# A blocked triangular inverse in which the matrix engine's level loop starts half a level later

## The chip, the cores and the metric

The kernel runs on one core of one Trainium2 chip. The metric is the device time of one execution in microseconds. Before the change it is 2102.54 us, the median of 3 runs (2102.18 to 2102.79).

## The reference

A decoder trunk of two layers over 512 positions of width 1024: in each layer a half-weighted SwiGLU feed-forward, a mixer, and a second feed-forward. The even layer's mixer joins a gated linear recurrence with RWKV-7 time mixing. The latter keeps a matrix state for each of 8 heads of width 64:

```
def step(state, inp):
    r_t, w_t, k_t, v_t, kk_t, a_t = inp
    sa = einsum('bhvk,bhk->bhv', state, kk_t)
    state = (state * w_t[:, :, None, :] - sa[..., None] * (kk_t * a_t)[:, :, None, :]
             + v_t[..., None] * k_t[:, :, None, :])
    return state, einsum('bhvk,bhk->bhv', state, r_t)
```

The odd layer's mixer is a gated delta rule, which the change doesn't touch.

## The kernel before

The RWKV recurrence is computed in 8 chunks of 64 tokens. In a chunk it needs the inverse of a unit lower triangular 64x64 matrix, for 8 heads and 8 chunks. Heads go in two **rounds** (`q` = 0, 1) of two **streams** (`z` = 0, 1); a stream is one 128x512 tile, that is 16 blocks of 64x64 with two heads across the partitions. The inverse is built by doubling: **levels** of block size 2, 4, ... 64. A level of a stream is this chain:

- TensorE, `pe_level_u` (products at L725): 32 products 64x64 of the running inverse `XX` with the triangle `TM`, into the lower half of two PSUM banks;
- VectorE, `level_masked` (L2065): the result times a mask, into `IU`; ahead of it on VectorE stands `turned_across` (L2055 and L2057), three transposes of `XX` into `XT`;
- TensorE, `pe_level_xx` (L735): 32 products of `XT` and `IU`, into the upper half of the banks;
- ScalarE, `level_copied` (L1396): the copy of these into `XX`. The next level's products and transposes wait for it.

The last level has `pe_last_xx` (L744) in place of the second product. In the text u(z,l) and x(z,l) are the two products of stream z at level l.

Beside this chain TensorE does other products of the same round: `back_product` (L882), the **inner products** `inside_inner` (L891) and the **outer products** `inside_outer` (L902; these use banks 2 and 3 for stream 0, 6 and 7 for stream 1). ScalarE copies the outer results away in two copies for each stream (`inside_copied`, L1403), and signals `token_read`. In the loop TensorE also turns a staged tile of keys (`tokens_turned`, L692, called T(l) here) into the lower half of banks 2 and 3, so it first waits for `token_read[0]`; ScalarE copies that (`tokens_copied`, L1391), and GpSimd stages the next tile (`stage`, L1915). In round 0 ScalarE has two more copies in each of levels 1 and 2 (`branch_hi`, L1386).

The order on every engine is written out by hand, once for both rounds. TensorE's, from the middle of a round: back product 0, u(0,1), first x of stream 1, back product 1, inner 0, inner 1, outer 0, outer 1, wait for `token_read[0]`; then a hardware loop over l = 1 to 3 (`pe.Fori`) of u(1,l), x(0,l), T(l), u(0,l+1), x(1,l). ScalarE copies the results of the first x products, then inside 0 and inside 1, and then goes through the levels. VectorE's order isn't changed. After the rounds comes a scan over the chunks, whose first products wait for the last copies of both streams. Each 64x64 product is two instructions, a weight load and a matmul. TensorE's code outside `Fori` loops is straight-line.

Of the kernel before, what the change touches and what calls it, by code (L numbers as in the profile page):

```python
# [147 lines left out]
def hybrid_trunk_kernel(nc, x, params, const, w_gate, w_up, w_down, ab_in, ab_out, lru_a, lru_x,  # L148
# [28 lines left out]
    with ExitStack() as ctx:  # L177
# [423 lines left out]
        def _(pe):  # L601
# [87 lines left out]
            def tokens_turned(first, src, b, upper, across):  # L689

                for r, a, c in four_ways:
                    tr = pe.matmul(head_block(first, a if across else r, c, upper), src[r, b, c * CHUNK:(c + 1) * CHUNK],  # L692
                                   con("ident")[r, r], start=True, stop=True)
                tr.then_inc(tr_mm, 1)
# [24 lines left out]
            def pe_level_u(q, z, l):  # L719

                w = INV[z]
                pe.wait_ge(xx_read[z], 5 * q + l)
                pe.sem_inc(level_begun, 1)
                for a, f, c in four_ways:
                    mm = pe.matmul(head_block(4 * z, f, c), w["TM"][a, c, :], w["XX"][a, c, :], start=True, stop=True)  # L725
                mm.then_inc(u_mm[z], 1)

            def pe_level_xx(q, z, l):

                w = INV[z]  # L730
                pe.wait_ge(iu_ready[z], 5 * q + l + 1)
                pe.wait_ge(xt_turned[z], 4 * q + l)
                pe.sem_inc(level_begun, 1)
                for a, f, c in four_ways:
                    mm = pe.matmul(head_block(4 * z, a, c, upper=True), w["XT"][f, c, :], w["IU"][f, c, :], start=True, stop=True)  # L735
                mm.then_inc(xx_mm[z], 1)

            def pe_last_xx(q, z):
# [5 lines left out]
                    mm = pe.matmul(head_block(4 * z, crossed(r) if z else r, c, upper=True), w["IU"][r, c, :], w["XT"][r, c, :], start=True, stop=True)  # L744
                mm.then_inc(xx_mm[z], 1)

            def mix_out(phase, ready):

                n, c = norm_of[phase], base[phase] + AB_BLOCKS

                def rows_of(m, rows, wait):

                    more = (MORE_HI[:, m - 2], MORE_LO[:, m - 2]) if m in (2, 3) else None
                    unit(BANK[4 + m] if m < 4 else DOWN[m % 2], c + m, 0, (MIX_HI, MIX_LO), rows, rows[0] == 0, rows[-1] == KB - 1,
                         ready=ready if wait else None, at_col=rows[0], done=rows[-1] == KB - 1, weights=more)

                pe.wait_ge(logs_ready, 4)
                for m in range(4):
                    rows_of(m, range(4), m == 0)
                for m in range(2):  # L760
                    rows_of(m, (4, 5, 6), m == 0)
                for m in range(2):
                    rows_of(m, (7,), m == 0)
                for m in range(2, 4):
                    rows_of(m, range(4, KB), False)
                for m in range(4, KB):
                    pe.wait_ge(x_ready[m % 2], KB // 2 * (n + 1) + (m // 2 if m >= 6 else 1))
                    rows_of(m, range(KB), False)

            for phase in plan:  # L770
                if phase.startswith("ffn"):
                    q = ffn_index[phase] * (FB // 2)
# [17 lines left out]
                if phase == "ab":  # L790
# [94 lines left out]
                    def inside_inner(q, z):  # L885

                        b = 2 * q + z
                        pe.wait_ge(mat_ready[z], 4 * q + 4)
                        for r, a, c in four_ways:
                            cc = slice(c * CHUNK, (c + 1) * CHUNK)  # L890
                            mm = pe.matmul(head_block(4 * z + 2, crossed(r) if z else r, c), TKM[z][a, c, :], VT[a, b, cc], start=True, stop=True)  # L891
                        if z:
                            mm.then_inc(inner_mm, 1)
# [11 lines left out]
                    for q in range(2):  # L905
                        if q == 0:
                            triangle_product(0, 0)
                            triangle_product(0, 1)
                        if q == 0:
                            key_products(q, 0)  # L910
                            key_products(q, 1)
                            pe.wait_ge(bv_ready, 2)
                            tokens_turned(4, KF, 0, upper=False, across=True)
                            pe_first_u(q, 0)
                        else:
                            pe_first_u(q, 0)
                            key_products(q, 0)
                            key_products(q, 1)
                            pe.wait_ge(xx_read[1], 5)
                            tokens_turned(4, AL, 0, upper=False, across=False)  # L920
                        pe_first_xx(q, 0)
                        pe_first_u(q, 1)
                        back_product(q, 0)
                        pe_level_u(q, 0, 1)
                        pe_first_xx(q, 1)
                        back_product(q, 1)
                        inside_inner(q, 0)
                        inside_inner(q, 1)
                        inside_outer(q, 0)
                        inside_outer(q, 1)  # L930
                        pe.wait_ge(token_read[0], 2 * q + 2)
                        with pe.Fori(1, 4) as l:
                            pe_level_u(q, 1, l)
                            pe_level_xx(q, 0, l)
                            pe.wait_ge(tr_read, l + 4 * q + 4)
                            pe.wait_ge(staged, l + 3 * q)
                            pe.sem_inc(level_begun, 1)
                            tokens_turned(2, STAGE, 0, upper=False, across=q == 0)
                            pe_level_u(q, 0, l + 1)
                            pe_level_xx(q, 1, l)  # L940
                        if q == 0:
                            triangle_product(1, 0)
                        pe_level_u(q, 1, 4)
                        pe_last_xx(q, 0)
                        if q == 0:
                            triangle_product(1, 1)
                        pe_last_xx(q, 1)
# [383 lines left out]
        def _(act):  # L1331
# [74 lines left out]
            def act_inverse(q):  # L1406

                tokens_copied((KT, BT)[q], 0, 4, False, 4 * q + 5)
                level_copied(q, 0, 0)
                level_copied(q, 1, 0)  # L1410
                inside_copied(q, 0)
                inside_copied(q, 1)
                for l in range(1, 4):
                    level_copied(q, 0, l)
                    tokens_copied((KT, BT)[q], l, 2, False, 4 * q + 5 + l)
                    level_copied(q, 1, l)
                    if q == 0 and l in (1, 2):
                        branch_hi(2 * l - 2)
                        branch_hi(2 * l - 1)
                level_copied(q, 0, 4)  # L1420
                level_copied(q, 1, 4)
# [1273 lines left out]
```

## Time and profile before

| | us |
|---|---|
| median of the runs | 2102.54 |
| span of the profiled execution | 2102.0 |
| TensorE busy in the span | 2062.4 (98%) |
| VectorE, ScalarE, GpSimd busy | 1131.0, 780.5, 160.7 |
| round 0, first masks to last copy | about 513 to 547 |
| round 1, to the last copy | about 547 to 576 |

The median of the runs is 0.5 us above the profiled span; of the profiled execution nothing but its span is recorded. The busy shares are of the whole span. The page's 40 slices hold 52.6 us each, so both rounds lie in one or two of them, and the stage has to be read from the timeline.

### The profile page before, as it was taken

Reading aid. Unit: us, or ns where it says so; the run is one execution under the profiler, and the core shown is the slowest. Engines: PE = TensorE matmul, PEld = TensorE weight load, DVE = VectorE, ACT = ScalarE, POOL = GpSimd, SP = SyncE. Lnnn points to the kernel's source line nnn. Section 1 sums busy time; section 2 is a strip of 40 time slices with the busy share of each in tenths; the row PEclk is TensorE's granted clock in tenths of the full one; section 3 lists DMA queues with packets and bytes.
Section 4 is the critical chain, followed back from the end, with each engine's and each line's share of the span. In section 5 each row is a group of like instructions: output and inputs, shape, how many; then the busy total and the mean of one; then the engine's idle time right before and its main releaser. Section 6 shows DMA issues by size and latency. Waiting matters only on the chain.

```text
span 2102.0 us, 33182 instructions
## 1 busy us (share of the span) xinstructions
PE 2062.4 (98%) x13322; PEld 1699.5 (81%) x13322; DVE 1131.0 (54%) x1463; ACT 780.5 (37%) x1182; POOL 160.7 (8%) x118
## 2 busy tenths in 40 slices
PE   8999999999799999999999999999999999999998
PEld 6888888777768888888888888877888888888886
DVE  6444444678767444444444443469777675444322
ACT  5233223483434223322323232246665453233221
POOL 0000011002302000011000001101111120000010
PEclk9999999999999999999999999999999999999999
DMA  5222322320022222322222232221111122222321
GB/s 183 100 93 97 113 96 81 106 78 14 11 74 91 100 99 91 115 97 89 91 94 95 100 109 98 86 80 62 51 51 42 58 86 99 100 90 100 111 97 52
DMA packets 48265, 182.65 MB, mean 87 GB/s; under 512 B 6320, under 2 KB 6576, under 8 KB 48048
## 3 DMA queue, kind: packets, MB, share of 16 engines
q1 hardware_dynamic: 48176, 181.39, 25.1%
q8 instruction: 65, 1.06, 0.2%
q14 instruction: 24, 0.20, 0.0%
HBM read 179.27 MB, written 2.10 MB: 86 GB/s over the span
## 4 chain that ended last, share of the span: by engine, by line
PE 69%; DVE 2%; ACT 1%; issue 0%; POOL 0%; DVEq 0%; ACTq 0%; POOLq 0%
PE banks L614 21%; PE banks L615 21%; PE banks L616 21%; PE banks L1225 1%; PE banks L1194 0%; PE banks L1176 0%; PE banks L1264 0%; PE banks L1047 0%; PE banks L1266 0%; PE banks L1245 0%; PE banks L1242 0%; PE banks L1150 0%; PE banks L1130 0%; PE banks L1006 0%; DVE WS L1989 0%
## 5 line engine op out<-in xcount | busy, mean ns | idle before, releaser
L614 PE MATMUL banks<-H,WS 128*128 128x512 f32 x1840 | 727.6, 395 | 8.4 <-DVE H L2073 8.0
L615 PE MATMUL banks<-H,WS 128*128 128x512 f32 x1840 | 717.0, 390 | 0.0
L616 PE MATMUL banks<-H,WS 128*128 128x512 f32 x1840 | 716.9, 390 | 0.0
L1340 ACT ACTIVATE WS<-RAW 128x1024 fp32r<-128x1024 f32 (+1 forms) x306 | 345.0, 1128 | 909.4 <-PE banks L616 905.5
L1989 DVE TENSOR_TENSOR WS<-RAW,WS 128x1024 fp32r<-128x1024 f32 (+1 forms) x306 | 400.9, 1310 | 193.6 <-ACT WS L1340 193.2
L614 PEld LDWEIGHTS banks<-H,WS 128*128 128x128 f32 x1840 | 345.7, 188 | 85.1 <-DVE WS L1989 9.2
L616 PEld LDWEIGHTS banks<-H,WS 128*128 128x128 f32 x1840 | 345.7, 188 | 72.5
L615 PEld LDWEIGHTS banks<-H,WS 128*128 128x128 f32 x1840 | 345.9, 188 | 70.2 <-issue 1.2
L614 PE MATMUL banks<-A,WS 128*128 128x512 f32 x704 | 273.9, 389 | 0.0
L616 PE MATMUL banks<-A,WS 128*128 128x512 f32 x704 | 273.9, 389 | 0.0
L615 PE MATMUL banks<-A,WS 128*128 128x512 f32 x704 | 273.9, 389 | 0.0
L2029 DVE TENSOR_TENSOR US<-banks,RSTD 128x512 f32<-128x512 f32 x88 | 60.8, 691 | 252.2 <-PE banks L616 252.2
L1855 POOL TENSOR_TENSOR ACC<-ACC,US 128x512 f32<-128x512 f32 x47 | 87.5, 1862 | 1402.5 <-issue 763.0
L2029 DVE TENSOR_TENSOR GS<-banks,RSTD 128x512 f32<-128x512 f32 x88 | 60.8, 691 | 179.9 <-PE banks L616 179.8
L614 PEld LDWEIGHTS banks<-A,WS 128*128 128x128 f32 x704 | 132.1, 188 | 27.5
L616 PEld LDWEIGHTS banks<-A,WS 128*128 128x128 f32 x704 | 132.1, 188 | 27.5
L615 PEld LDWEIGHTS banks<-A,WS 128*128 128x128 f32 x704 | 132.1, 188 | 27.3
L2001 DVE SCALAR_TENSOR_TENSOR X<-banks,X 128x512 f32 (+1 forms) x48 | 33.0, 688 | 159.2 <-PE banks L616 159.2
L1380 ACT ACTIVATE A<-US 128x512 f32 (+1 forms) x88 | 55.8, 634 | 46.9 <-DVE US L2036 46.6
L2036 DVE TENSOR_TENSOR US<-GS,US 128x512 f32<-128x512 f32 x88 | 60.9, 692 | 9.1
L2041 DVE TENSOR_TENSOR A<-US,A 128x512 f32 (+1 forms) x88 | 60.2, 685 | 2.8 <-ACT A L1380 2.8
L1375 ACT ACTIVATE GS<-GS 128x512 f32<-128x512 f32 x88 | 54.1, 615 | 10.7 <-DVE GS L2029 10.7
(406 smaller groups left out, 1657.6 us busy)
## 6 DMA issues: line engine op xcount, KB each, us to landing
RAW<-in_w_gate SPq DMA_DIRECT2D x88, 512.0 KB, 3.2
RAW<-in_w_up SPq DMA_DIRECT2D x88, 512.0 KB, 3.2
RAW<-in_w_down SPq DMA_DIRECT2D x64, 704.0 KB, 4.0
RAW<-in_c_in SPq DMA_DIRECT2D x32, 512.0 KB, 3.2
RAW<-in_ab_in SPq DMA_DIRECT2D x22, 512.0 KB, 3.2
RAW<-in_ab_out SPq DMA_DIRECT2D x8, 512.0 KB, 5.0
RAW<-in_c_out SPq DMA_DIRECT2D x8, 512.0 KB, 3.2
X<-in_x SPq DMA_DIRECT2D x4, 512.0 KB, 7.5
```

The costliest lines, as they stand in the source:

```text
L614: pe.matmul(bank[:, :], high[:, cols], upper, start=first and j == 0, stop=False)
L615: pe.matmul(bank[:, :], high[:, cols], lower, start=False, stop=False)
L616: mm = pe.matmul(bank[:, :], low[:, cols], upper, start=False, stop=last and j == len(rows) - 1)
L1340: act.activation(WS[:, 0, c % SPLIT, 0:cols] if dst is None else dst, RAW[:, c % RING, 0:cols], ACT.Copy).then_inc(hi_ready, 1)
L1375: act.activation(GS[:, j, :], GS[:, j, :], ACT.Silu).then_inc(silu_ready[j], 1)
L1380: act.activation(A[:, 0, 2 * i + j, :], US[:, j, :], ACT.Copy).then_inc(ahi_ready[j], 1)
L1855: pool.tensor_tensor(ACC[:, :], ACC[:, :], US[:, j, :], ALU.add).then_inc(acc_ready[j], 1)
L1989: vec.tensor_tensor(WS[:, 1, c % SPLIT, 0:cols], RAW[:, c % RING, 0:cols], WS[:, 0, c % SPLIT, 0:cols].bitcast(F32), ALU.subtract).then_in ...
L2001: vec.scalar_tensor_tensor(X[:, 2 * i + j, :], bank[:, :], factor, X[:, 2 * i + j, :], ALU.mult, ALU.add).then_inc(x_ready[j], 1)
L2029: vec.tensor_tensor((GS, US)[k][:, j, :], (GATE, UP)[k][j][:, :], RSTD[:, :], ALU.mult).then_inc((gs_ready, us_ready)[k][j], 1)
L2036: vec.tensor_tensor(US[:, j, :], GS[:, j, :], US[:, j, :], ALU.mult).then_inc(prod_ready[j], 1)
L2041: vec.tensor_tensor(A[:, 1, 2 * i + j, :], US[:, j, :], A[:, 0, 2 * i + j, :].bitcast(F32), ALU.subtract).then_inc(act_ready[j], 1)
```

## The change

```diff
@@ TensorE @@
+            def stage_turned(q, l):
+                pe.wait_ge(tr_read, l + 4 * q + 4)
+                pe.wait_ge(staged, l + 3 * q)
+                pe.sem_inc(level_begun, 1)
+                tokens_turned(2, STAGE, 0, upper=False, across=q == 0)
...
                         inside_inner(q, 0)
+                        pe_level_u(q, 1, 1)
+                        pe_level_xx(q, 0, 1)
                         inside_inner(q, 1)
                         inside_outer(q, 0)
                         inside_outer(q, 1)
                         pe.wait_ge(token_read[0], 2 * q + 2)
-                        with pe.Fori(1, 4) as l:
-                            pe_level_u(q, 1, l)
-                            pe_level_xx(q, 0, l)
-                            pe.wait_ge(tr_read, l + 4 * q + 4)
-                            pe.wait_ge(staged, l + 3 * q)
-                            pe.sem_inc(level_begun, 1)
-                            tokens_turned(2, STAGE, 0, upper=False, across=q == 0)
+                        with pe.Fori(1, 3) as l:
+                            stage_turned(q, l)
                             pe_level_u(q, 0, l + 1)
                             pe_level_xx(q, 1, l)
+                            pe_level_u(q, 1, l + 1)
+                            pe_level_xx(q, 0, l + 1)
+                        stage_turned(q, 3)
+                        pe_level_u(q, 0, 4)
+                        pe_level_xx(q, 1, 3)
@@ ScalarE, act_inverse @@
                 level_copied(q, 1, 0)
-                inside_copied(q, 0)
-                inside_copied(q, 1)
                 for l in range(1, 4):
                     level_copied(q, 0, l)
+                    if l == 1:
+                        inside_copied(q, 0)
                     tokens_copied((KT, BT)[q], l, 2, False, 4 * q + 5 + l)
                     level_copied(q, 1, l)
+                    if l == 1:
+                        inside_copied(q, 1)
                     if q == 0 and l in (1, 2):
                         branch_hi(2 * l - 2)
                         branch_hi(2 * l - 1)
```

The products u(1,1) and x(0,1) of both rounds now stand between the two inner products, ahead of the wait for `token_read[0]`. That wait now stands ahead of T(1). The loop body holds the same five groups in the same cyclic order and begins with T(l); it runs twice, and its third pass is written out but for the two groups that went ahead. On ScalarE the copy of x(0,1) goes ahead of inside 0, and inside 1 goes behind the copy of x(1,1). The work is the same.

## Rows read from the trace of the kernel before

**Rows 1.** Busy time by stretch: length, engines' busy us, TensorE's clock, DMA share, GB/s.
```profile
529.00:546.00 17.00, 12.36 (x642) 11.43 (x640) 13.84 (x28) 9.43 (x18) 9.09 (x9) 1.00 0.01 2
519.60:522.90 3.30, 3.30 (x67) 3.30 (x67) 1.60 (x3) 0.60 (x1) 3.30 (x4) 0.51 0.00 0
```

**Rows 2.** Timeline, round 0, head and first pass: start, us, work, idle before.
```profile
525.46 0.60 ACT L1396 ACTIVATE XX<-banks 128x512 f32<-128x512 f32 x1 [3.53 <-PE banks L716]
526.04 0.69 DVE L2065 TENSOR_TENSOR IU<-banks,CST 128x512 f32<-128x512 f32 x1
526.18 0.63 PE L891 MATMUL banks<-VT,TKM 64*64 64x64 f32 x30
527.38 0.69 PE L891 MATMUL banks<-VT,TKM 64*64 64x64 f32 x32 [0.57 <-DVE MBT L2291]
527.90 1.11 PE L902 MATMUL banks<-MKM,VT 64*64 64x64 f32 x64
528.63 0.60 ACT L1403 ACTIVATE GT<-banks 128x512 f32<-128x512 f32 x1 [2.57 <-PE banks L902]
529.12 0.59 ACT L1403 ACTIVATE YI<-banks 128x512 f32<-128x512 f32 x1
...
530.05 0.69 PE L725 MATMUL banks<-XX,TM 64*64 64x64 f32 x32 [1.04 <-ACT YI L1403]
530.81 0.69 DVE L2065 TENSOR_TENSOR IU<-banks,CST 128x512 f32<-128x512 f32 x1 [2.22 <-PE banks L725]
531.19 0.46 PE L735 MATMUL banks<-IU,XT 64*64 64x64 f32 x16 [0.21 <-issue]
532.35 0.45 DVE L2055 STREAM_TRANSPOSE XT<-XX 128x256 f32<-128x256 f32 x1 [0.85 <-ACT XX L1396]
```

**Rows 3.** Timeline, round 0, one turn of the level loop.
```profile
533.68 0.60 ACT L1396 ACTIVATE XX<-banks 128x512 f32<-128x512 f32 x1 [0.86 <-PE banks L735]
534.17 1.14 ACT L1386 ACTIVATE YA_HI<-GG 128x512 fp32r<-128x512 f32 x2
534.33 0.43 DVE L2055 STREAM_TRANSPOSE XT<-XX 128x256 f32<-128x256 f32 x1
534.42 0.69 PE L725 MATMUL banks<-XX,TM 64*64 64x64 f32 x32 [0.80 <-ACT XX L1396]
534.90 0.68 PE L735 MATMUL banks<-IU,XT 64*64 64x64 f32 x32
535.64 0.60 ACT L1396 ACTIVATE XX<-banks 128x512 f32<-128x512 f32 x1 [0.33 <-PE banks L735]
535.71 0.69 DVE L2065 TENSOR_TENSOR IU<-banks,CST 128x512 f32<-128x512 f32 x1
536.32 0.43 DVE L2055 STREAM_TRANSPOSE XT<-XX 128x256 f32<-128x256 f32 x1
```

**Rows 4.** Timeline, round 1: head, first pass, second pass.
```profile
552.40 1.04 PE L882 MATMUL banks<-FACTORS,AL 64*64 64x64 f32 x30
555.66 0.63 PE L891 MATMUL banks<-VT,TKM 64*64 64x64 f32 x30
556.87 0.69 PE L891 MATMUL banks<-VT,TKM 64*64 64x64 f32 x32 [0.57 <-DVE MBT L2291]
...
560.78 0.62 PE L735 MATMUL banks<-IU,XT 64*64 64x64 f32 x26 [0.43 <-issue]
563.40 0.60 ACT L1396 ACTIVATE XX<-banks 128x512 f32<-128x512 f32 x1 [0.43 <-PE banks L735]
565.16 1.15 PE L692 MATMUL banks<-CST,STAGE 64*64 64x64 f32 x32
566.11 0.68 PE L725 MATMUL banks<-XX,TM 64*64 64x64 f32 x32
```

**Rows 5.** Instruction-fetch DMAs (count, MB, share): whole span, then 531.2 to 560.7 us.
```profile
q8 instruction: 65, 1.06, 0.2%
q8 instruction: 6, 0.10, 1.4%
```

## The prediction

> **What bounds the kernel now.** I read the busy shares by slice first; they say only that the two rounds of the inverse are short and TensorE not full there. In the 17 us of round 0's loop and what follows it TensorE is busy 12.4, VectorE 13.8, ScalarE 9.4 [rows 1]: no engine bounds it alone, a chain does. The timeline shows which. One half level is: ScalarE's copy `XX` ends (534.28), u of one stream starts 0.14 later, x of the other stream 0.48 after that, x lasts 0.68, the copy starts 0.06 later and lasts 0.60: 1.96 us, and the copies of rows 3 are 1.96 apart. VectorE's round (transposes, then `IU`) repeats every 1.99 us (534.33, 536.32) with no idle time in a row [rows 3]. Both chains are full; the loop can't be made faster by reordering, only started earlier. Before the loop there is room: in round 0 u(1,1) starts at 530.05, though the copy it needs ended at 526.06; it is merely behind the wait for `token_read[0]`, and TensorE idled 1.04 us, VectorE 2.22 waiting for it and 0.85 at the next transposes [rows 2].
>
> A second thing limits the head. TensorE stops in the middle of x(0,1), where no semaphore stands: in round 0 after 16 of the 32 pairs (the last 16 start at 531.19), in round 1 after some 7 (26 matmuls are left at 560.78) [rows 2, 4]. From stop to stop there are 24 groups of 64 instructions less 9 pairs, and by the code some 18 single waits and register instructions: 1536. In that time six instruction fetches run; the page's 65 fetches bring 1.06 MB, 16 KB each [rows 5]. 1536/6 = 256 instructions per fetch, so both stops lie on a border between fetched blocks: the code isn't there yet. Counting 256 back from the stops by the listing, the previous border was passed 18 pairs into inner 1 of round 0 (about 527.65) and 10 pairs into it in round 1 (about 557.0). So the next block was usable 3.54 and 3.76 us after the border before it. I take 3.6 as the price of a block in straight-line code. Groups of four-way products go at about 0.48 us per 66 instructions [rows 3], 1.9 us per block, and so outrun it.
>
> The Trainium skill (Runtime: NRT & Kernel Launch, Instruction fetch mechanics) has the same 16 KiB blocks of 256 instructions, but calls the cost of crossing one "mostly hidden". By that sentence the new order would run without stops; that is rival A, worked out below from rows. The two stops speak against it here.
>
> **The change part by part.**
>
> Moved, u(1,1) and x(0,1) between the inner products. Everything they need is ready: the `IU` of stream 0 ends at 526.73 [rows 2]. u(1,1) at 526.65, x(0,1) at 527.1, inner 1 at 527.6 (its own wait had ended by 527.38), outer 0 at 528.0. They cost nothing: the same 64 pairs were done later. VectorE does `IU`(1,1) right behind its transposes at 528.5, then the transposes for u(0,2), whose copy ScalarE makes at 527.9. The 2.22 us wait goes. What is late next is `token_read[0]`: outer 0 to the first copy was about 0.75, the two copies take 1.1, and from their end (529.71) to TensorE's next product it is 0.34 [rows 2]; T(1) has one more single instruction (0.1, an estimate). So T(1) at 530.4 at the earliest, u(0,2) 0.5 later, x(1,1) 0.48 later, its copy ending at 532.8 against 534.28. Behind the wait on TensorE stand T(1) and everything of the level loop; VectorE's `IU`(0,2) and, through x(1,1), both streams wait for it. Gain at this point 1.5 us.
>
> Now the code fetch. The instruction positions do not change up to outer 1, so the border that was 18 pairs into inner 1 falls 18 pairs into u(1,1): 526.9. The next one, 256 on, falls 17 pairs into outer 1, usable at 526.9+3.6 = 530.5, where without a stop TensorE would be at 528.8. The rest of outer 1 and the waits: T(1) at 530.95 instead of 530.4, u(0,2) 531.4, x(1,1) 531.9 to 532.6, copy to 533.25: gain 1.0.
>
> ScalarE in round 0. Inside 1 (1.1 us) now stands behind that copy, and `branch_hi` (1.14) behind it; the copy of x(0,2) can't start before 533.2+1.1+1.1 = 535.5, ending at 536.1, against 536.24 [rows 3]. Before, the two `branch_hi` fitted with 0.33 to spare; now 1.1 is in the way. What is left of round 0's gain is 0.2 us; without the fetch stop the same sum gives 0.85. A further border, in u(1,2), costs nothing: usable at 534.1, x(0,2) done at 535.1, before ScalarE is free. GpSimd's stages follow `branch_hi` and T(l), which both move along; I take them at nothing.
>
> Round 1. The code grew: two groups were peeled ahead of the loop and three behind, about 330 instructions, which moves all borders of round 1 by 330-256 = 74 instructions against the work. They now fall 7 pairs into back product 0 (552.65), 7 pairs into inner 0, and 6 pairs into outer 0. Inner 0 would be there at 555.7 [rows 4]; the block is usable at 552.65+3.6 = 556.25; the next at 559.85, in outer 0, which without a stop would start at 557.5. So outer 0's end moves from 558.0 to 560.4, its two copies end at 561.6, T(1) starts at 562.05, u(0,2) 1.0 later (round 1's T is long, 1.15, [rows 4]), and x(1,1)'s copy ends at 564.85 against 564.00: a loss of 0.85 where the plain count promises a gain of 1.45. Inside 1 on ScalarE costs nothing here: no `branch_hi` in this round, and from the end of that copy (564.00) to the one that u(0,3) waits for there was some 1.3 us.
>
> The loop border. It stood between x(1,l) and u(1,l+1), where TensorE waited 0.80 [rows 3]; now it stands ahead of T(l+1). No row times a branch; bounds 0 to 0.80, I take 0.3, since the second loop's exit and entry show nothing larger. The Trainium skill (Advanced Engine Details and Errata, Control Flow Timing) gives about 0.1 us for a compare-and-branch; no row here shows one, and with it the sum would be 0.2 lower. In round 0 T takes no longer than a u (x(0,2) at 534.90, so T(2) at 535.4, issued by 535.9), and u(0,3) waits for the copy's end at 536.24 anyway: that covers it. In round 1 u(0,3) starts as T(2) ends (565.16+0.95 = 566.11) [rows 4], so all of it is lost: 0.3. The loop exit, ahead of T(3), costs 0.1 more.
>
> **The sum.** Round 0: -0.2. Round 1: +0.85+0.3+0.1 = +1.25. Together +1.05; TensorE's sequencer runs up to 0.3 us ahead of the products when nothing makes it wait, which brings each border forward, and the range of the block's price (3.54 to 3.76) does little more, so I take +0.8: span 2102.8, and with the 0.5 between span and median, 2103.3 us. After the rounds everything hangs on the last copy and shifts with it, weights too.
>
> The bounds: without any fetch stop, round 0 -0.85, round 1 -1.45+0.4, or -1.9 in all; with 3.76 per block and a branch of 0.8, +1.9.
>
> **Rivals.** The measurement tells a difference from no change above 0.2%, 4.2 us; all of the above is inside.
>
> A, the code is there in time (fetches run ahead by more than I count): -1.9, 2100.6 us. For it: elsewhere borders pass without a stop. Against: the two stops and the count of 256. 0.22.
>
> B, the stop belongs to the first pass of a hardware loop, not to the block: it then falls in T(1) or u(0,2), 0.4 to 0.6 us in each round: -0.2 in round 0 and -0.5 in round 1, 2101.8 us. For it: both stops are in a first pass. Against: they are at different pairs. 0.13.
>
> C, slower: TensorE's clock. From 519.6 to 522.9 it was at half (0.51, the 1.2 GHz level) [rows 1], in round 0 after TensorE had stood waiting twice; round 1's same stretch was at full clock. If the stop in outer 0 (2.3 us of idle) brings such a stretch to round 1, its 3.3 us cost at most 1.65 more: 2105.0 us. It is decided by whether the clock falls after about 559. To pass +0.2% it would have to happen twice besides my sum. 0.10.
>
> D, the change doesn't do what it says, u(1,1) being held by something else than its place: 2102.5. All its inputs' rows end before 526.8. 0.02.
>
> My forecast, 0.53. Range 2100.5 to 2104.6: it holds A, B, and the forecast with its bounds, and leaves most of C out. Faster by over 0.2% needs twice rival A: 0.03. Slower by over 0.2%, C twice: 0.04. Within it: 0.93.
>
> **What would show it.** T(1) ahead of everything in the loop, at 530.9 in round 0 (530.4 by A). A stop in the middle of outer 1 in round 0, after 17 pairs, and in round 1 short in inner 0, then of 2 us after 6 pairs of outer 0. VectorE's waits for u(1,1) gone. ScalarE without idle time from the copy of x(1,1) to that of x(0,2) in round 0. The last `XTF` copy 0.8 us later than before. Wrong if outer 0 and outer 1 run through in round 1, or if a stop's place is not 256 instructions from the one before.

## The result, and the profile after

| us | before | after |
|---|---|---|
| median | 2102.24 (19 runs, 2101.47 to 2103.36) | 2106.37 (19 runs, 2102.87 to 2109.32) |
| span of the profiled execution | 2102.0 | 2104.6 |

The change costs time: the ratio is 1.0018 (95%: 1.0012 to 1.0024), and the medians lie 4.1 us apart. The forecast was 2103.3, and 2106.4 is above its range. After also spreads over three times as wide as before (6.5 us against 1.9).

The page tells as little as before did. Its first lines, and the number of instruction fetches (65 in [rows 5]):

```profile
span 2104.6 us, 33172 instructions
PE 2063.5 (98%) x13322; PEld 1701.2 (81%) x13322; DVE 1131.9 (54%) x1463; ACT 781.1 (37%) x1182; POOL 160.8 (8%) x118
...
q8 instruction: 67, 1.10, 0.2%
```

TensorE is busy 1.1 us longer; the rest is in the gaps, and those stand in the timeline. Round 0 of the kernel after, to set beside [rows 2, 3] (start, us, engine, line, work, idle time before):

```profile
526.42 0.64 PE L898 MATMUL banks<-VT,TKM 64*64 64x64 f32 x31
526.84 0.92 PE L909 MATMUL banks<-MKM,VT 64*64 64x64 f32 x49
...
529.26 0.46 PE L909 MATMUL banks<-MKM,VT 64*64 64x64 f32 x15 [1.50 <-issue]
529.63 0.69 PE L692 MATMUL banks<-CST,STAGE 64*64 64x64 f32 x32
...
530.85 0.69 DVE L2076 TENSOR_TENSOR IU<-banks,CST 128x512 f32<-128x512 f32 x1 [1.69 <-PE banks L725]
531.32 0.60 ACT L1405 ACTIVATE XX<-banks 128x512 f32<-128x512 f32 x1 [0.33 <-PE banks L735]
...
532.06 0.46 PE L725 MATMUL banks<-XX,TM 64*64 64x64 f32 x14 [0.80 <-ACT XX L1405]
532.77 1.16 ACT L1395 ACTIVATE YA_HI<-GG 128x512 fp32r<-128x512 f32 x2
533.48 0.50 PE L725 MATMUL banks<-XX,TM 64*64 64x64 f32 x17 [0.97 <-issue]
534.56 0.60 ACT L1405 ACTIVATE XX<-banks 128x512 f32<-128x512 f32 x1 [0.63 <-PE banks L735]
534.68 1.14 PE L692 MATMUL banks<-CST,STAGE 64*64 64x64 f32 x32 [0.17 <-issue]
535.55 1.11 PE L725 MATMUL banks<-XX,TM 64*64 64x64 f32 x32
536.41 1.11 PE L735 MATMUL banks<-IU,XT 64*64 64x64 f32 x32
537.58 0.60 ACT L1405 ACTIVATE XX<-banks 128x512 f32<-128x512 f32 x1 [1.11 <-PE banks L735]
```

Three things can be read here. TensorE stops in the middle of a group twice, and "issue" says that no semaphore holds it: 49 matmuls of L909 are 32 of outer 0 and 17 of outer 1. The `XX` of x(1,1) comes at 531.32, well ahead of the 533.68 of [rows 3]: the head start exists. And from 534.68 on a group takes 1.11 us instead of 0.68 to 0.69: TensorE's clock. The copies at 534.56 and 537.58 are 3.02 us apart instead of 1.96.

Round 1 of the same kernel:

```profile
557.40 0.33 PE L909 MATMUL banks<-MKM,VT 64*64 64x64 f32 x6
559.09 1.14 PE L909 MATMUL banks<-MKM,VT 64*64 64x64 f32 x58 [1.35 <-issue]
559.80 0.60 ACT L1412 ACTIVATE GT<-banks 128x512 f32<-128x512 f32 x1 [1.97 <-PE banks L909]
...
561.36 1.48 PE L692 MATMUL banks<-CST,STAGE 64*64 64x64 f32 x30 [1.13 <-ACT YI L1412]
563.87 0.69 DVE L2076 TENSOR_TENSOR IU<-banks,CST 128x512 f32<-128x512 f32 x1 [3.90 <-PE banks L725]
564.72 0.60 ACT L1405 ACTIVATE XX<-banks 128x512 f32<-128x512 f32 x1 [1.14 <-PE banks L735]
...
565.95 0.68 PE L735 MATMUL banks<-IU,XT 64*64 64x64 f32 x32
566.91 1.09 PE L692 MATMUL banks<-CST,STAGE 64*64 64x64 f32 x30 [0.29 <-issue]
```

The `XX` of x(1,1), at 563.40 in [rows 4], is now at 564.72. The same two places as windows (length, busy us of TensorE's matmuls and weight loads, VectorE, ScalarE, GpSimd, then the clock):

```profile
534.86:538.27 3.41, 2.66 (x96) 2.47 (x94) 2.08 (x5) 1.59 (x4) 1.69 (x2) 0.54 0.00 0
562.16:565.57 3.41, 2.60 (x84) 2.44 (x84) 0.91 (x2) 1.45 (x3) 2.26 (x2) 0.54 0.02 5
```

Both are at the 1.2 GHz level but for their ends. What before had at 519.6 [rows 1] is gone here. The last copies `XTF` of both rounds stood at 546.16 and 575.29 before; after:

```profile
546.08 0.60 ACT L1405 ACTIVATE XTF<-banks 128x512 f32<-128x512 f32 x1 [1.59 <-PE banks L744]
...
577.01 0.60 ACT L1405 ACTIVATE XTF<-banks 128x512 f32<-128x512 f32 x1 [0.68 <-PE banks L744]
```

Behind the rounds, in the scan over the chunks, there is one more stop, in a group that ran through before:

```profile
585.97 0.56 PE L1015 MATMUL banks<-GT,KBT 64*64 64x64 f32 x10
587.39 0.38 PE L1015 MATMUL banks<-GT,KBT 64*64 64x64 f32 x5 [0.86 <-issue]
...
587.94 0.42 DVE L2358 TENSOR_TENSOR SH<-SDEC,banks 128x256 f32<-128x256 f32 x1 [2.20 <-PE banks L1015]
```

It costs 1.17 us, compared instruction by instruction with before. So on the profiled spans: -0.1 to the end of round 0, +1.8 in round 1, +1.2 in the scan, 2.9 together (2.6 between the spans; the two executions begin some 0.15 us apart and differ by 0.3 at the very end). Round 0's -0.1 flatters the change: the profiled before carried the half-clock stretch at 519.6, and after did not. VectorE's instructions, the same in both, stand 0.14 us later in after at 518.7 and 1.40 us earlier at 526.0, so the stretch cost the profiled before 1.5 us.

### The profile page after: what moved, and what is told of

It reads as the page before. It is cut to its first block, busy times and chain, and to the rows that moved or that the text cites. A ratio compares the mean times of both kernels' runs of the same rounds, so it can differ in the third digit from the quotient of the medians.

```text
span 2104.6 us, 33172 instructions
## 1 busy us (share of the span) xinstructions
PE 2063.5 (98%) x13322; PEld 1701.2 (81%) x13322; DVE 1131.9 (54%) x1463; ACT 781.1 (37%) x1182; POOL 160.8 (8%) x118
## 4 chain that ended last, share of the span: by engine, by line
PE 69%; DVE 2%; ACT 1%; issue 1%; POOL 0%; DVEq 0%; ACTq 0%; POOLq 0%
PE banks L614 21%; PE banks L615 21%; PE banks L616 21%; PE banks L1234 1%; PE banks L1203 0%; PE banks L1185 0%; PE banks L1273 0%; PE banks L1056 0%; PE banks L1275 0%; PE banks L1254 0%; PE banks L1251 0%; PE banks L1159 0%; PE banks L1139 0%; PE banks L1015 0%; DVE HF L2686 0%
## 5 line engine op out<-in xcount | busy, mean ns | idle before, releaser
L1384 ACT ACTIVATE GS<-GS 128x512 f32<-128x512 f32 x88 | 54.1, 615 | 10.8 <-DVE GS L2040 10.8
```

Of the source, the lines that this page charges most:

```text
L1384: act.activation(GS[:, j, :], GS[:, j, :], ACT.Silu).then_inc(silu_ready[j], 1)
```

## The experiments

Each median is of 9 to 11 runs, timed beside the kernel before (its median 2102.0 to 2102.3 every time); e5 and e6, further down, are one execution each. The length of a stop is given as in the rows, as TensorE's idle time.

| kernel | median us | ratio, 95% |
|---|---|---|
| e1 before, third pass written out | 2107.14 | 1.0012 to 1.0032 |
| e2 after, ScalarE's order of before | 2107.22 | 1.0019 to 1.0037 |
| e3 only u(1,1) ahead, loop of three passes | 2106.99 | 1.0014 to 1.0032 |
| e4 after, 128 instructions ahead | 2108.2 | 1.0018 to 1.0038 |
| e7 after, weight loads later | 2107.71 | 1.0017 to 1.0036 |
| e8 before, outer 1 twice | 2108.1 | 1.0018 to 1.0038 |
| e9 after, stop filled with products | 2107.18 | 1.0014 to 1.0032 |
| e10 after, loop border in a wait | 2107.18 | 1.0016 to 1.0034 |
| e11 before, 128 instructions ahead | 2105.43 | 1.0006 to 1.0025 |
| e12, e13 before, 64 and 192 ahead | 2105.86, 2103.1 | 1.0009 to 1.0027, 0.9996 to 1.0014 |
| e14, e15 after, 64 and 192 ahead | 2107.25, 2105.3 | 1.0014 to 1.0033, 1.0006 to 1.0025 |

**The length of the code alone.**

```diff
-                        with pe.Fori(1, 4) as l:
+                        def level_pass(q, l):
...
+                        with pe.Fori(1, 3) as l:
+                            level_pass(q, l)
+                        level_pass(q, 3)
```

> The order of before on every engine; only the loop runs two passes and its third pass (five groups, about 330 instructions) is written out behind it. Theory (code fetch: a block of 256 instructions is usable some 3.3 to 3.8 us after the border before it was passed): round 0 is as before, with the stop 16 pairs into x(0,1). In round 1 the borders move by 74 instructions as in the changed kernel, to 7 pairs into inner 0 and 7 pairs into u(1,1), where TensorE waits for token_read anyway, so round 1 has no stop there and its loop starts up to 0.5 us earlier. In the scan the border stands where it stands in the changed kernel (10 pairs into the fourth-chunk products at L1015 there), and its fetch meets the weight loads: a stop of about 1.1 us. Sum: -0.5 + 1.1, so +0.6 us, 2102.9. Rival (the moved products and their order cost the time, not the code): no difference from before, no stop in the scan, 2102.3.

2107.14, where 2102.9 was expected. The order of the work is that of before; only the third pass of the loop is written out. This costs as much as the whole change, 5.0 us. The border 7 pairs into u(1,1) caused no stop in round 1, as expected. But the next one, 256 instructions on, falls behind the first pair of x(1,1), and I hadn't counted that far (the rows are T(1), u(0,2) and x(1,1)):

```profile
560.54 1.15 PE L692 MATMUL banks<-CST,STAGE 64*64 64x64 f32 x32
561.49 0.69 PE L725 MATMUL banks<-XX,TM 64*64 64x64 f32 x32
561.97 0.22 PE L735 MATMUL banks<-IU,XT 64*64 64x64 f32 x1
563.79 0.69 PE L735 MATMUL banks<-IU,XT 64*64 64x64 f32 x31 [1.60 <-issue]
```

Others stand in the written pass and behind it (0.3 to 0.5 us), and one of 1.7 us in the scan at 586.5. The stop that the profiled before has in round 0's x(0,1) doesn't show here: the group runs through in 0.67 us. The clock has no part in this execution (length, busy us and clock from before the rounds into the scan):

```profile
512.00:600.00 88.00, 67.62 (x2744) 61.45 (x2742) 56.70 (x113) 26.47 (x48) 30.13 (x26) 1.00 0.09 28
```

Its span of 2106.0 is nevertheless 5.6 us above the 2100.4 of a median run of before; about 1 us of that arises ahead of the rounds, by comparison with the profiled before. The order of the products isn't needed to explain a loss of this size, and neither is half clock; the borders between fetched blocks are enough.

**ScalarE's order.**

```diff
                 level_copied(q, 1, 0)
+                inside_copied(q, 0)
+                inside_copied(q, 1)
                 for l in range(1, 4):
                     level_copied(q, 0, l)
-                    if l == 1:
-                        inside_copied(q, 0)
...
```

> The changed kernel, with ScalarE's order of before: both streams' inside copies ahead of the copy of x(0,1). Theory: outer 1 is stopped by the code fetch until 529.3 in round 0 and outer 0 until 559.1 in round 1, and the copy of x(0,1) now stands behind outer 1: it ends near 531.7 in round 0 (529.9 + 1.1 + 0.6) instead of 527.25, u(0,2) waits for it, so T(1) is as early but u(0,2) 1.4 later; the two inside-1 copies are out of the way of branch_hi, which gives 0.5 back. About +1 us on the changed kernel in each round. Rival (ScalarE's new order is what costs time): 1 to 2 us less than the changed kernel.

2107.22. The copy of x(0,1) now waits on ScalarE behind inside 1, and that for the interrupted outer 1; u(0,2) needs it:

```profile
531.38 0.60 ACT L1405 ACTIVATE XX<-banks 128x512 f32<-128x512 f32 x1
...
532.13 1.13 PE L725 MATMUL banks<-XX,TM 64*64 64x64 f32 x32 [1.17 <-ACT XX L1405]
```

In after that copy stands at 526.65 and u(0,2) at 530.12. Of these 2.0 us 0.6 are no loss of the order: this execution is that much behind after from ahead of the rounds. The remaining 1.4, as expected, are 1.1 at round 0's last copy (547.82), 0.4 at round 1's (578.06), and 0.85 between the medians, whose intervals overlap. Half clock differs too (one stretch of 6.8 us from 531.3 on). So ScalarE's new order looks like the better one for the new TensorE order, by up to a microsecond that the medians don't resolve, and it isn't where the 4 us went.

**The same start without longer code.** Only u(1,1) goes ahead, and the loop keeps three passes: x(0,l), T(l), u(0,l+1), x(1,l), u(1,l+1).

```diff
                         pe_level_u(q, 1, 1)
-                        pe_level_xx(q, 0, 1)
...
+                        with pe.Fori(1, 4) as l:
+                            pe_level_xx(q, 0, l)
+                            pe.wait_ge(token_read[0], 2 * q + 2)
...
-                        stage_turned(q, 3)
-                        pe_level_u(q, 0, 4)
-                        pe_level_xx(q, 1, 3)
```

> Only u(1,1) is moved ahead of inner 1; the loop keeps three passes, x(0,l), T(l), u(0,l+1), x(1,l), u(1,l+1), so the code is no longer than before and all borders of round 1 and of the scan stay where before has them. The wait for token_read stands behind x(0,l). ScalarE copies inside 0, then x(0,1), then inside 1. Theory: in both rounds the stop is some 18 and 9 pairs into x(0,1), ending near 530.0 and 559.8, T(1) right behind it, no stop in the scan: 1 to 2.5 us faster than before, 2100 to 2101.3, and some 5 us faster than the changed kernel. Rival (half clock follows any closer packing of the head): slower than before like the changed kernel.

2106.99: wrong by over 5 us, and it is the most instructive miss. It still has the stops (1.2 us in x(0,1) and 0.7 in u(1,2) in round 0, 1.1 and 0.7 in the same two groups of round 1), since they hang on positions and not on the number of instructions. It has none in the scan, as expected. And the loop's border now lies between u(1,l+1) and x(0,l+1), on the chain:

```profile
536.08 0.69 PE L725 MATMUL banks<-XX,TM 64*64 64x64 f32 x32 [0.31 <-ACT XX L1400]
...
538.04 0.69 PE L725 MATMUL banks<-XX,TM 64*64 64x64 f32 x32 [0.80 <-ACT XX L1400]
538.90 0.77 PE L735 MATMUL banks<-IU,XT 64*64 64x64 f32 x32 [0.17 <-issue]
539.48 0.69 PE L692 MATMUL banks<-CST,STAGE 64*64 64x64 f32 x32
540.47 0.29 PE L725 MATMUL banks<-XX,TM 64*64 64x64 f32 x4 [0.29 <-ACT XX L1400]
```

x follows u by 0.86 instead of 0.48, and a pass takes 4.39 us (536.08 to 540.47) instead of twice 1.96.

**The blocks moved against the code.** 128 single increments of an unused semaphore stand in TensorE's code of the input projection, eight behind each of 16 groups, where its queue runs well ahead of the products; no delay is seen there.

```diff
+                        if 2 <= t < 18:
+                            for _ in range(8):
+                                pe.sem_inc(padding, 1)
```

> The changed kernel with 128 single increments of an unused semaphore on TensorE, 8 behind each of 16 dense units of the even mixer's input projection, where the matmuls (0.23 us apart) hide them. Nothing else changes but that all later borders between code blocks fall 128 instructions earlier in the work. Theory: the stops move from 17 pairs into outer 1 (round 0) to 17 pairs into inner 1 and 16 pairs into u(0,2), and from 6 pairs into outer 0 (round 1) to 6 pairs into x(0,1) and the start of T(1); the stop in the scan moves or goes. Rival (the stops belong to places of the program, such as the outer products): they stay in outer 1 and outer 0. Time within 2 us of the changed kernel.

2108.2. The stops moved by half a block, to the places named ahead: inner 1 and u(0,2) in round 0, and in round 1 6 pairs into x(0,1) (0.4 us) and the start of T(1) (0.2). Round 0's:

```profile
525.60 0.45 PE L902 MATMUL banks<-VT,TKM 64*64 64x64 f32 x17
527.53 0.40 PE L902 MATMUL banks<-VT,TKM 64*64 64x64 f32 x12 [1.47 <-issue]
...
530.45 0.44 PE L726 MATMUL banks<-XX,TM 64*64 64x64 f32 x15
531.40 0.50 PE L726 MATMUL banks<-XX,TM 64*64 64x64 f32 x17 [0.51 <-issue]
```

The scan's stop was gone. This shows what the stops are: they stay with the 256-instruction blocks when the work moves against them.

**Both kernels once more, one execution each.**

> The kernel before, unchanged, for a second profile. Of its runs so far 27 of 29 had a span near 2100.4 and no lower clock than 0.998; the profile that the prediction used had a span of 2102.0 and 3.4 us at half clock in round 0. Expected: span 2100 to 2101, TensorE at full clock from 512 to 577, the stops again 16 and 7 pairs into x(0,1).

> The changed kernel, unchanged, for a second profile. Expected: the stops at the same pairs (17 pairs into outer 1, 13 or 14 pairs into u(1,2), 6 pairs into outer 0, 10 pairs into L1015 in the scan), since they hang on the code; stretches at half clock in other places or none, since its runs differ by 6 us with the clock. Span 2101 to 2107.

Before: 2103.51, span 2101.7, where 2100 to 2101 at full clock was expected: it has a half-clock stretch again, at 519.3. Its stop in round 1's x(0,1) is there (0.6 us behind 6 pairs); round 0's is all but gone, the group takes 0.85 us instead of 0.68. After: 2111.07, span 2109.3, with its stops at the same pairs, longer (2.0 us in outer 1 and in outer 0), one of 0.8 us in inner 0, where the forecast had one, and this in its windows:

```profile
536.10:539.50 3.40, 2.60 (x108) 2.45 (x106) 2.47 (x6) 1.70 (x4) 1.13 (x2) 0.55 0.00 0
563.40:573.60 10.20, 8.96 (x256) 8.72 (x256) 4.58 (x9) 3.37 (x6) 2.87 (x3) 0.52 0.01 2
```

The places of the stops are fixed; their lengths and the clock aren't. Where products set the pace, the 6.8 us more at half clock can cost up to 3.4 of the 4.7 us between this execution and the first.

**The weight loads out of the way of the scan's fetch.**

```diff
                                 sp.wait_ge(xx_mm[s], 10)
+                            sp.wait_ge(solve_mm, 4)
                         load(u0 + j, (u0 + j) % RING, *units[u0 + j])
```

> The changed kernel; the first loads of the output projection's weights wait also for the fourth chunk's solve (about 587) instead of going at the end of the inverse (577.4). Theory: the stop at L1015 in the scan (585.97 + 0.9 idle) comes from its instruction fetch, which was 3.4 us late behind these 2 MB; with the loads gone from there that stop shrinks below 0.3 us and may come back at a later border, where a fetch then meets the loads. The stops in the rounds stay. Within 1.5 us of the changed kernel, either side. Rival (the stop belongs to the code's length alone): it stays at that pair.

2107.71. The stop behind 10 pairs of L1015 is gone, and another came with the moved loads:

```profile
587.44 0.68 PE L1016 MATMUL banks<-GT,KBT 64*64 64x64 f32 x16
...
596.41 0.44 PE L1009 MATMUL banks<-GT,XTF 64*64 64x64 f32 x10 [0.16 <-DVE GT L2346]
598.17 0.28 PE L1009 MATMUL banks<-GT,XTF 64*64 64x64 f32 x3 [1.32 <-issue]
```

So that stop is a fetch held up by data loads. In after the last border ahead of it was passed at about 581.7, and the fetch shows only at the end of the loads (queues in 585.0 to 585.3: packets, MB, share):

```profile
q1 hardware_dynamic: 12, 0.04, 33.5%
q8 instruction: 1, 0.02, 20.3%
```

None is recorded from 582 to 585, 3.4 us behind the border; elsewhere in the rounds it starts 0.7 to 2.2 us behind it. In e7 that same fetch starts at 583.24, within 0.1 us of its border, and the fetch that now meets the loads starts 3.6 us behind its own (592.2, then 595.8). Moving the loads moves the loss and doesn't save it: by VectorE's instructions e7 gives up 1.6 us there.

**More products in idle time.** Before, with outer 1 computed twice; TensorE waits for `token_read[0]` there anyway.

```diff
                         inside_outer(q, 0)
+                        inside_outer(q, 1, last=False)
                         inside_outer(q, 1)
```

> The kernel before with the outer products of stream 1 done twice (same values written), 64 more instructions and 0.5 us of TensorE in each round, in a place where TensorE waits 1.04 us for token_read. Rival (the head is bound by the waits): hidden, no difference, 2102.2. Theory (the head is bound by code fetch): TensorE stops again at the same instruction, now 17 pairs into u(1,1) in round 0, until about the same time (531.2); everything behind it is 64 instructions, 0.5 us, later, and the loop's first pass now reaches one border more, in x(1,1), a stop of 1 us: +1.5 to +2.5 us in each round, and the borders of round 1 and the scan move by another 64: 2104.5 to 2107.

2108.1, +6 us and above the expected 2104.5 to 2107, for 32 pairs (about 0.5 us) in each round, in idle time. The pairs moved the borders into u(1,1) (0.6 us) and x(1,1) (1.5 us) in round 0 and into u(0,2) of round 1 (1.1 us). "Free" work in the idle time of an engine isn't free where it is code.

**The stop filled.** In after, inner 1 runs two (round 0) and three times (round 1) in a loop of its own, so that TensorE stands still for less time.

```diff
-                        inside_inner(q, 1)
+                        with pe.Fori(0, FILL[q]) as _:
+                            inside_inner(q, 1)
```

> The changed kernel with inner 1 done twice in round 0 and three times in round 1, in a small hardware loop of its own (same values written), just ahead of the stops in outer 1 and outer 0. TensorE works in what was idle, the code behind is fetched meanwhile. Theory (half clock follows the idle time that the stops make): T(1) within 0.5 us of the changed kernel in both rounds, and the granted clock of most runs 0.998 instead of 0.995 to 0.998; median 2105 to 2106. Rival (the clock falls for the work's kind, whatever the idle time): as many runs at 0.995 to 0.997 as the changed kernel has (13 of 19), median 2106.4 or more.

2107.18, with 3 of 11 runs at the mean clock 0.998 that before nearly always has; after has 6 of 19. The profiled run had full clock in both rounds, but over the runs nothing improved. That idle time lowers the clock isn't shown by this, nor refuted: stops remained (in round 0 1.1 us in outer 1, 0.7 in u(1,2) and 0.7 behind it, in round 1 0.6 in outer 0).

**The border of the loop back in a wait.** The first pass written out, then a loop over l = 2 and 3 in the order of before.

```diff
-                        with pe.Fori(1, 3) as l:
+                        stage_turned(q, 1)
+                        pe_level_u(q, 0, 2)
+                        pe_level_xx(q, 1, 1)
+                        with pe.Fori(2, 4) as l:
+                            pe_level_u(q, 1, l)
+                            pe_level_xx(q, 0, l)
```

> The changed kernel with the same order of work, but the written-out pass is the first (T(1), u(0,2), x(1,1)) and the loop holds u(1,l), x(0,l), T(l), u(0,l+1), x(1,l) for l = 2, 3, as before has it: the loop border stands again where TensorE waits 0.8 us for ScalarE's copy. Theory: the 0.4 us that the branch costs ahead of T(2) in round 1 comes back, the code is as long as in the changed kernel, so the stops stay where they are: 0.3 to 0.6 us less than the changed kernel, 2106. Rival (the branch costs nothing): no difference. The noise of either, some 0.5 us on a median, is as large; the trace tells it.

2107.18. The pause at T(2) in round 1 is gone, and the profiled span is 2103.6, 1.0 us below that of after. By VectorE's instructions 0.35 of that lie in round 1; the other 0.7 are the scan's stop, 0.23 us long here. Over 11 runs the median is no better, and none of them reached the clock 0.998. The border's 0.4 us are real in the trace and too small to be seen under the spread of the runs.

**Where the kernel before happens to stand.** The same padding in before; then 64 and 192 instructions (4 and 12 for each group) in either kernel.

> The kernel before with the 128 hidden single instructions of the padded kernel: no work in the rounds is changed or moved, only where the borders fall. Theory: the stops go from x(0,1) to some 50 instructions into outer 0 or 1 and some 15 pairs into u(0,2) in round 0, in round 1 into outer 1 and the first pairs of u(0,2); the scan's borders move too. Time between 1 us less and 3 us more than before, with the stops at those places. Rival (code position does not matter where the order is unchanged): 2102.2, stops in x(0,1).

> The kernel before with 64 hidden single instructions (4 behind each of 16 dense units). Borders fall 64 earlier: round 0's stop 5 pairs into u(1,1), round 1's 9 instructions into the token wait or u(1,1), and one border more inside the loop's first pass, some 28 instructions before its end, in x(1,1), with a stop of 1 to 2 us in each round. Position theory: 2104 to 2106. Rival (128 was a special case, the order decides): 2102.2.

> The kernel before with 192 hidden single instructions. Borders 192 earlier: in inner 1 and, 256 on, in T(1) or x(0,1)'s end, where the fetch is 1 to 2 us late: 2103.5 to 2106 by the position theory, 2102.2 by the rival.

> The changed kernel with 64 hidden single instructions: stops in outer 0 (round 0), in x(1,1) of the first pass, in inner 1 (round 1). If position is all, the four positions of both kernels have about the same mean (2104 to 2106) and this one may be anywhere in 2103 to 2108; if the change costs by itself, it is over 1.5 us above the kernel before with 64.

> The changed kernel with 192 hidden single instructions: stops in x(0,1)'s first half and in T(1) (round 0), in inner 0's end or u(1,1) and x(0,1) (round 1). As with 64: by the position theory 2103 to 2108 without a fixed distance to the kernel before with 192, otherwise over 1.5 us above it.

Stops of before with 128 (first two rows) and with 64 instructions (last two), in round 0:

```profile
531.92 0.46 PE L726 MATMUL banks<-XX,TM 64*64 64x64 f32 x14 [0.33 <-ACT XX L1400]
533.65 0.50 PE L726 MATMUL banks<-XX,TM 64*64 64x64 f32 x18 [1.28 <-issue]
```

```profile
531.72 0.44 PE L736 MATMUL banks<-IU,XT 64*64 64x64 f32 x14
533.51 0.56 PE L736 MATMUL banks<-IU,XT 64*64 64x64 f32 x18 [1.35 <-issue]
```

| instructions ahead | 0 | 64 | 128 | 192 | mean |
|---|---|---|---|---|---|
| before | 2102.2 | 2105.9 | 2105.4 | 2103.1 | 2104.2 |
| after | 2106.4 | 2107.3 | 2108.2 | 2105.3 | 2106.8 |

Position alone moves before by up to 3.7 us and after by up to 2.9. The unpadded before is the best of its four places. After is slower at each of them, by 4.1, 1.4, 2.8 and 2.2, on the mean 2.6. At 64, 128 and 192 the intervals of the two kernels overlap, so no single one of these three differences is firm; that of the four together is (95%: 1.7 to 3.0, by drawing the runs anew). So of the 4.1 us measured, about 1.5 are the luck of before's place, and 2.6 came with the change at the four places tried. What in the change costs them, its longer code, its loop border or its order, wasn't separated at the other places. e3 to e10 aren't faster than after in the median either, and no version here beats before.

## Why the prediction was wrong

Three terms of the sum failed: the scan, put at nothing and measured at 1.2 us; half clock, left out of the sum and present in both rounds; and the border in u(1,2), put at nothing. The steps one by one:

**The mechanism** was right. Both stops of round 0 are where the count put them (17 pairs into outer 1, and in u(1,2) behind 14), and so is the long one of round 1 (6 pairs into outer 0); the one in inner 0 didn't show in this execution, but did in e6. The first ended at 529.26. The forecast's 530.5 is in the time of the profiled before, whose stage begins 1.4 us later, so it was met within 0.2. The one in outer 0 ended at 559.09 instead of 559.85, since the stop in inner 0 ahead of it didn't come. The one in u(1,2) ended at 533.48, where 534.1 less 1.4 was forecast, 0.8 us too late: the fetch's price isn't one number. Counted back 256 instructions in the traces it was 3.6, 4.2 and 3.5 us for these three, 3.3 to 4.5 over all straight stretches with a stop, and at most 3.1 in e1, where round 0's x(0,1) ran through. The Trainium skill (Runtime: NRT & Kernel Launch, Instruction fetch mechanics) calls the cost of a crossing "mostly hidden"; in this stage the trace doesn't agree, with stops of 0.97 to 1.50 us of idle time, and rival A, which rested on the same idea, is out. So is rival B: the stops of after are in outer 1 and outer 0, ahead of the loop. e4 and e12, where padding moved the stops to places named ahead, show that the stops belong to the blocks. The 0.3 us by which the sequencer was taken to run ahead of the products, one reason for taking 0.8 instead of 1.05, is in no row.

**The moved work** was costed right: inner 1 begins at 526.42, x(1,1)'s copy came 2.4 us earlier than before (1.0 without the 1.4 by which the stage starts earlier; forecast 1.0), and VectorE's wait for u(1,1) is gone. What is late next is VectorE's wait for u(0,2), 1.69 us in round 0 and 3.90 in round 1, both at the end of a fetch stop.

**Round 0, forecast -0.2.** The last copy came at -0.1, but by another way. "ScalarE in round 0" failed: it isn't the limit. The copy of x(0,2) was ready to run 0.63 us before its products ended, because the stop in u(1,2) (0.97), which I had costed at nothing, came first; then half clock took another 1.1 us. And without the stretch at 519.6, after started this stage 1.4 us ahead of the profiled before. Against a before without that stretch, round 0 loses about 1.3, so the -0.1 is luck. (The forecast's 0.85 without a fetch stop was also misadded: with the copy's end at 532.8, the same sum gives 0.6.)

**Round 1, forecast +1.25.** T(1) at 561.36 instead of 562.05, but then the copy of x(1,1) starts 3.36 us after it instead of 2.2, at half clock: +1.3 at this point instead of +0.85. The border cost 0.42 (T(2) is 0.96 behind x(0,2), where 0.54 is normal) instead of 0.3. In all +1.8. The Trainium skill (Advanced Engine Details and Errata, Control Flow Timing) gives about 0.1 us for a compare-and-branch; the trace doesn't agree, its record of the one at this border (566.34) lasts 0.22 us, and register instructions of the turn stand around it.

**The scan, forecast 0.** "After the rounds everything hangs on the last copy and shifts with it, weights too" failed: it cost 1.17 us. The loads shift with the copy, but the blocks move against the work, and a border fell where 2 MB of loads held the fetch back (e7). In before a fetch is held back as long under the same loads (border at about 576.9, fetch at 579.98), and no stop comes of it there.

**Clock, rival C, given 0.10.** By the mean clocks this is what spreads after's runs and lifts their median. At clock 0.998 are 6 of the 19, with a mean of 2104.1 us; at 0.997, 0.996 and 0.995 they are at 2106.0, 2107.6 and 2108.8. The mean clock counts stretches only roughly, since the last 6.7 to 10.8 us of every profiled execution are at half clock too: e13 reads 0.997 with full clock throughout the rounds. I had priced one stretch, in round 1, and gave two 0.04; both profiled executions of after have two, one in each round, and [rows 1] had shown that round 0 can have one.

**The base** hid the others. "The 0.5 between span and median" was no constant: in every execution for which both are known, but for four of e9, time less span is 1.7 to 1.9 us. The profiled before therefore took about 2103.8, not its median 2102.5: it had the half-clock stretch, which few timed runs of it can have had (32 of 33 in the last comparison are at 0.998, and the median run's span is 2100.4). The two slips, 1.5 too much in the span and 1.3 too little behind it, nearly cancel, so they cost the forecast only 0.3. [rows 1] was read as a property of the kernel; both profiled executions of before have the stretch, but by its span the median run hasn't. From the right base the forecast was 2102.2 + 0.8 = 2103.0; with the scan's 1.2, 2104.2, which is what the runs of after at 0.998 have (2104.1). The rest, 2.2 us, goes to the clock. In the profiled execution the two half-clock passages cost 1.1 and 1.2 us more than forecast (3.02 instead of 1.96, and 3.36 instead of 2.2), which fits. That last sum is argued: no execution of after at 0.998 was profiled, and it isn't the only possible split: the profiled e1, e3, e4 and e11, all at full clock in the rounds, have spans 4.2 to 5.6 us above that of a median run of before. There the stops do it without half clock; -0.4 to 1.4 us of it arise ahead of the rounds.

**Open:** what lowers the clock. It falls in stages where TensorE stands waiting and starts again, and by the mean clock the changed kernels nearly all have it more often; but e9, with less idle time, didn't have it less often, and e14, with long stops (1.9 us in round 0), is at 0.998 in 8 of 11 runs. Open too is why a fetch takes 3.1 us at one border and 4.5 at another.

## What to carry to other kernels

Where short products run in straight-line code, instruction fetch can be the bound: count the instructions between unexplained stops, and before a hardware loop is peeled, unrolled or shifted, count where every border will fall afterwards, through to the stages behind. Before an edit worth a few microseconds is credited or blamed, time both kernels with a few hidden no-operations ahead of the place; here that alone moved the time by as much as the edit. And compare the span and clock of the profiled execution with those of the timed ones before any sum is made on it.

## What the runs showed of the hardware

- 256 instructions of 64x64 products (a weight load and a matmul each) take about 1.9 us to execute at full clock, and the next block was usable 3.3 to 4.5 us behind the border (in e1 once within 3.1); stops of 0.2 to 2.0 us. From the fetch's DMA to the first product of its block it is 2.2 to 2.9 us (in the scan 585.1, then 587.39).
- Under 2 MB of weight loads on the other queue a fetch's DMA started 3.1 to 4.2 us behind its border (before, after, e7, e1); when the loads were moved away it started within 0.1 us of it (e7).
- TensorE turns from one pass of a hardware loop to the next at a cost of about 0.4 us where nothing covers it (0.38 in e3, 0.42 in round 1 of after). The record of the taken compare-and-branch lasts 0.21 to 0.22 us, that of the last one, which leaves the loop, 0.08.
- Half-clock stretches in the rounds came as 3.4 us, once as 6.8 (e2) and once as 10.2 (e6). Over executions of one program they come and go: by the mean clock, a rough count, 1 in 33 of before's runs in the last comparison fell below 0.998, and 13 in 19 of after's.
